# Down projection: the low parts of the weights made by an accumulating DMA onto ACT's negative high parts, in place of a subtraction on DVE

## The reference

```python
def swiglu(h, w_gate, w_up, w_down):
    return (jax.nn.silu(h @ w_gate) * (h @ w_up)) @ w_down
...
        x = x + swiglu(rmsnorm(x, norm2_g[l]), w_gate[l], w_up[l], w_down[l])
    return rmsnorm(x, norm_f_g)
```

## Time and profile before

| what | value |
|---|---|
| time, median of 3 runs | 798.29 us (797.98 to 798.69) |
| the profiled execution's own time | 798.42 us |
| its span | 796.5 us |
| mean granted clock of TensorE | 0.994 of full speed |
| PE busy | 779.7 us, 98% of the span |
| PEld, DVE, ACT, POOL busy | 640.6, 372.3, 254.4 and 24.4 us |
| the chain that ended last | PE 93%, DVE 2%, issue 2%, ACT, DMA and POOL 1% each |
| moved by DMA | 75.64 MB, mean 95 GB/s |

### The profile page before, as it was taken

The page is one execution under the profiler, slowest core; times in us unless marked ns, Lnnn a source line. Parts: engine busy times, 40 slices in busy tenths (PEclk is TensorE's granted clock), DMA queues, the critical chain, the costliest instruction groups (busy, mean ns, idle before and its releaser), DMA issues.

```text
span 796.5 us, 9542 instructions
## 1 busy us (share of the span) xinstructions
PE 779.7 (98%) x3851; PEld 640.6 (80%) x3851; DVE 372.3 (47%) x576; ACT 254.4 (32%) x421; POOL 24.4 (3%) x45
## 2 busy tenths in 40 slices
PE   6999999999899999999999999999999999999996
PEld 6988888788576788888889988888888888888885
DVE  4688434357777443342547434334443444223224
ACT  6444221244455332332333332332332233123111
POOL 4000000012100000000000000000000000000000
PEclk9999999999999999999999999999999999999999
DMA  8434333211111034332331332233332233332402
GB/s 227 122 103 136 129 106 105 62 46 53 54 54 39 16 106 159 106 105 106 109 103 54 107 98 69 98 106 106 105 107 89 74 103 107 115 96 66 146 0 107
DMA packets 61916, 75.64 MB, mean 95 GB/s; under 512 B 3680, under 2 KB 49840, under 8 KB 61872
## 3 DMA queue, kind: packets, MB, share of 16 engines
q1 hardware_dynamic: 61872, 75.02, 29.4%
HBM read 72.92 MB, written 2.10 MB: 94 GB/s over the span
## 4 chain that ended last, share of the span: by engine, by line
PE 93%; DVE 2%; issue 2%; ACT 1%; DMA 1%; POOL 1%; SPq 0%; POOLq 0%; DVEq 0%; ACTq 0%
PE bank L1148 29%; PE bank L1150 28%; PE bank L1149 28%; PE bank L1369 1%; PE bank L1337 1%; PE bank L1354 1%; DMA stage<-in_w_in 1%; PE bank L1298 1%; PE bank L1160 1%; PE bank L1311 1%; POOL head_rs L428 0%; PE bank L1344 0%; PE bank L1272 0%; PE bank L1291 0%; DVE hT_lo L710 0%
## 5 line engine op out<-in xcount | busy, mean ns | idle before, releaser
L1148 PE MATMUL bank<-hT_hi,w_hi 128*128 128x512 f32 (+1 forms) x680 | 261.4, 384 | 2.8 <-DVE hT_lo L710 2.4
L726 DVE TENSOR_TENSOR w_lo<-stage,w_hi 128x1024 fp32r<-128x1024 f32 x125 | 152.4, 1224 | 228.8 <-ACT w_hi L469 220.3
L1150 PE MATMUL bank<-hT_hi,w_lo 128*128 128x512 f32 (+1 forms) x680 | 257.1, 378 | 0.0
L1149 PE MATMUL bank<-hT_lo,w_hi 128*128 128x512 f32 (+1 forms) x680 | 257.0, 378 | 0.0
L469 ACT ACTIVATE w_hi<-stage 128x1024 fp32r<-128x1024 f32 x127 | 133.4, 1053 | 132.7 <-PE bank L1150 127.3
L1148 PEld LDWEIGHTS bank<-hT_hi,w_hi 128*128 128x128 f32 x680 | 128.8, 189 | 27.5 <-issue 3.0
L1150 PEld LDWEIGHTS bank<-hT_hi,w_lo 128*128 128x128 f32 x680 | 128.7, 189 | 23.9
L1149 PEld LDWEIGHTS bank<-hT_lo,w_hi 128*128 128x128 f32 x680 | 128.8, 189 | 21.8
L1148 PE MATMUL bank<-w_hi,aT_hi 128*128 128x512 f32 x176 | 68.5, 389 | 0.0
L1149 PE MATMUL bank<-w_lo,aT_hi 128*128 128x512 f32 x176 | 68.5, 389 | 0.0
L1150 PE MATMUL bank<-w_hi,aT_lo 128*128 128x512 f32 x176 | 68.5, 389 | 0.0
(11 more groups left out here) (175 smaller groups left out, 770.8 us busy)
## 6 DMA issues: line engine op xcount, KB each, us to landing
stage<-in_w_in SPq DMA_DIRECT2D x21, 1024.0 KB, 5.2
stage<-in_w_gate SPq DMA_DIRECT2D x11, 1024.0 KB, 5.4
stage<-in_w_up SPq DMA_DIRECT2D x11, 1024.0 KB, 5.3
stage<-in_w_down SPq DMA_DIRECT2D x22, 512.0 KB, 4.4
stage<-in_w_out SPq DMA_DIRECT2D x4, 1024.0 KB, 5.1
x_nat<-in_x SPq DMA_DIRECT2D x4, 512.0 KB, 5.4
stage<-in_w_br_mlstm SPq DMA_DIRECT2D x4, 512.0 KB, 3.5
stage<-in_w_br_fox SPq DMA_DIRECT2D x4, 512.0 KB, 4.5
```

Of the source, the lines that this page charges most:

```text
L726: dve.tensor_tensor(ring(w_lo, g), staged(g), ring(w_hi, g).bitcast(F32), ALU.subtract).then_inc(lo_split, 1)
L1148: pe.matmul(o, a_hi, b_hi, start=first, stop=False)
L1149: pe.matmul(o, a_hi, b_lo, start=False, stop=False)
L1150: return pe.matmul(o, a_lo, b_hi, start=False, stop=last)
```

## The change

For the 22 granules of the down projection DVE's subtraction is gone. ACT writes, right behind the high part, minus the same rounded value into `w_lo`, with one more activation of the same shape (scale -1.0), and counts it in a new semaphore `minus_hi`. POOL waits for that and issues a DMA which reads the granule from HBM a second time and adds it to what is in `w_lo`, so that `w_lo` becomes the weight minus its high part; its landing is counted in one of four semaphores `lo_landed`, one per ring buffer. PE waits for the landing in place of `lo_split`. SP waits for `minus_hi` in place of `lo_split` before it loads a staging buffer that held such granules. On POOL the 22 waits and DMAs stand between the roots of the second and of the third norm.

```diff
+        minus_hi = sem("minus_hi")
+        lo_landed = [sem(f"lo_landed{i}") for i in range(RING)]
...
+        def down_block(g):
+            half, f = down[g - G_DOWN]
+            return w_d[f * P:(f + 2) * P, half * HALF:(half + 1) * HALF].rearrange("(k p) c -> p k c", p=P)
+        def ring_count(g):
+            return (g - G_DOWN) // RING + 1
...
-                sp.wait_ge(lo_split, slots[s - STAGES][0])
+                freed_by = slots[s - STAGES][0]
+                if freed_by <= G_DOWN:
+                    sp.wait_ge(lo_split, freed_by)
+                else:
+                    sp.wait_ge(minus_hi, freed_by - G_DOWN)
                 load_slot(s)
...
             rows_rstd(1)
+            for g in range(G_DOWN, N_GRAN):
+                pool.wait_ge(minus_hi, g - G_DOWN + 1)
+                pool.dma_start(ring(w_lo, g), down_block(g), accum_op=ALU.add).then_inc(lo_landed[(g - G_DOWN) % RING], 16)
             rows_rstd(2)
...
                 act.activation(ring(w_hi, g), staged(g), ACT.Copy).then_inc(hi_split, 1)
+                if g >= G_DOWN:
+                    act.activation(ring(w_lo, g), staged(g), ACT.Copy, scale=-1.0).then_inc(minus_hi, 1)
...
             def split_lo(g):
-                if g >= N_GRAN:
+                if g >= G_DOWN:
                     return
...
-                    pe.wait_ge(lo_split, g + 1)
+                    pe.wait_ge(lo_landed[(g - G_DOWN) % RING], 16 * ring_count(g))
                     pe.wait_ge(aT_lo_ready, 2 * d + 2)
...
                     if r == 0:
-                        pe.wait_ge(lo_split, g + 1)
+                        pe.wait_ge(lo_landed[(g - G_DOWN) % RING], 16 * ring_count(g))
```

## The result

The changed kernel takes 805.99 us, the median of 3 runs (805.49 to 806.55), against 798.29 us before: a ratio of 1.01, with a 95% interval of 1.0085 to 1.0114. The profiled execution took 805.99 us with a span of 804.3 us, so 1.7 us lie around the span (1.9 before) and nothing new happens outside it. The forecast was 806.0.

A forecast was written before the change was run, and what follows sets the result against it. The prediction took PE to bound the kernel, with the removed subtractions hidden beside its work. End 4.5, start 1.5 and clock 1.6 summed to 7.6 us on the profiled 798.42, giving 806.0 us; range 800.5 to 824.

The forecast's parts named there:

- The reading of the bound: Down projection: PE bounds, DVE's removed subtractions lie beside its work; freeing 27 us of DVE and both edits are worth nothing.
- Term 1, the end: Before granule 21 in row block 0: PE idles 4.5 us, as 6.3 us meets 1.83 of slack; bounds 1.1 to 9.2.
- L: Time from the end of ACT's second activation to when PE may start; 6.3 us where no other DMA runs.
- Term 2, the start: At granule 1, its DMA beside SP's pair of loads: 8.2 us against 6.65 of slack, 1.5 us lost; bounds 0 to 4.4.
- Term 3, the clock: After the idle time at the end: one fall to half speed for some 3.2 us, 1.6 us lost; bounds 0 to 3.2.
- Throughput: Down projection's stream: adding DMA 3.3 us plus load 1.6, together 4.9 of 5.43 us per granule, fits but by little.
- rival 2: Down projection: DMAs become the bound if an add takes over 3.8 us of all engines; about 850 us; chance 0.17.
- The short landing: At granule 21: L at most 3.4 us, no clock fall, no change that can be told; 799.8 us; chance 0.06.
- A cost of POOL's first DMA: At granule 0 or around the span: own cost over 8.2 us, excess added to 806; with 10 us, 816; chance 0.06.
- Faster: Down projection: a gain from freeing DVE, though nothing waits for it here; no size given; chance 0.01.

## Why the prediction was right, step by step

**The reading of the bound held.** DVE lost 27 us and PE won none. ACT's second activation was hidden everywhere, and SP's changed wait cost nothing.

**Term 1, the end: 4.5 us forecast, 4.8 measured.** Row block 0 begins granule 18 at 769.65 us and granule 21 at 778.53, 8.88 us for 18 matmuls of 0.2266 us, 4.80 late. L was put at 6.3 us and was 6.34. It was built from a load of 1024 KB (5.2 us) and two short POOL instructions (1.1), and came out as 0.31 us to POOL's start and 6.03 from there, POOL's 1.20 included. So POOL's part was 1.5 us and the rest 4.8: the two pieces were off by 0.4 us each way, and that they cancel is luck. Granule 20's delay lay within granule 21's, as I had it. The missing 0.3 us is ACT's start on granule 21, 0.54 us behind PE's first matmul on granule 18, 0.26 before; the trace does not say why. Moving the place of use by 4.08 us took the wait from 4.01 to 0.54, which shows the cause.

**Term 2, the start: 1.5 forecast, 1.72 measured.** L was put at 8.2 and was 8.37. The 8.2 was picked between 6.3 and 11.0 with no row behind it, so its closeness is partly luck. That it comes from sharing with SP's pair of loads is shown by the run in which the DMA was alone (6.1 us), and that the place has only 6.65 us by the run in which the traffic hit granule 2 instead.

**Term 3, the clock: 1.6 forecast, 1.7 to 1.8 measured** in the profiled execution. The windows of the earlier trace rows, with the grant at 0.50 in those from 16 to 18 as well, add up to 3.4 us at half speed and a loss of 1.7, not 3.2 and 1.6; the fall behind granule 21 has the same size. Its cause is shown by the pair with and without filling matmuls. Its size was luck in part: nearly the same wait costs 3.4 us in other kernels' profiled executions. A sum of 8.4 less the 0.64 us by which this execution was ahead at 670 us made the 7.8; the agreement to 0.01 us is chance. The places of the two waits and the fall of the clock are not, and each has a run of its own behind it.

**Throughput: the conclusion was right and its working wrong.** I took the share of the DMA engines as work: 1.6 us for a plain load and twice that for an add, 4.9 of 5.43 us, and a threshold of 3.8 us for rival 2. The share did come out near 0.9, as foreseen, and yet another 524 KB per granule on top of it were hidden, and only the next 524 KB pushed it over. The term that fits all four kernels of this kind (plain, adding, one and two extra) is bytes read, with the tile that is added to, against about 405 GB/s: 3.9 of 5.43 us for the changed kernel. By that count rival 2 deserved less than its 0.17, and the range's upper end could have lain lower.

**The rivals.** The short landing (L under 3.4 us) did not come: even a plain DMA from POOL needed 4.2 us at granule 21. The fit of the Trainium skill (DMA: Bandwidth & Descriptors, "Anatomy of one DMA — SWDGE (gpsimd) path"), which makes an estimate of 3.2 us for these bytes, is under both the plain 4.2 and the adding 6.0 us, and the measurement decides. A cost of POOL's first DMA did not come either: 6.2 us at granule 0, and 1.7 us around the span. Faster did not come.

**Left open:** what decides whether a wait of about 2 us brings the clock down and how long it stays down; no run here separates it. Also open is whether 405 GB/s is the bound of all DMA engines or of POOL's queue.

## What to carry to other kernels

Taking work off an engine that nobody waits for gives nothing; what such a change moves is latency, so list for each buffer how long it has between coming free and being wanted, and compare the new way's time with the smallest of these, at the first and the last pass rather than in the steady stretch. An adding DMA is slow to land but cheap in a steady stream, and a change of the order in which the last buffers are wanted can hide it. Reckon a DMA stream by bytes read, the destination of an add included, and not by the share of the engines. Do not count on a late landing costing only its wait: behind waits of 2.8 to 4.3 us the clock fell each time and took 1.7 or 3.4 us more.

## What was not expected

- A share of the DMA engines of 0.92 left room for another 102 GB/s (198 to 300 GB/s) without one new wait, and at 1.07 both a stream that fits and one that does not look alike.
- The fall of the clock differs in length between the profiled executions of different kernels: 3.4 us at half speed in one, 6.8 in another, after waits of 4.01 and 3.92 us. A wait of 2.17 us near 677 us left the grant at 1.00, one of 2.22 us near 682 us was followed by a fall to 0.50 while PE was already at work again.
- An adding DMA issued 1.6 us ahead of the pair of loads was not slowed by them (6.2 us at granule 0, while granule 1's add behind them took 11.1); one issued 0.7 us ahead of four loads was (8.7 us at granule 2, against 6.0). Whether the lead or the number of loads matters is not shown.
- The first matmul after a wait takes 0.50 to 0.80 us in the trace, against 0.39 in the stream.
